# Gathering an expert's tokens straight into the transposed operand, in a hybrid decoder block with a mixture of experts

## The reference

```
h = rms_norm(x, g_ffn)
logits = h @ w_router + b_router             # 32 experts
top 4 of them, weights = softmax over the 4
per expert e, for the tokens that chose it:
    g = min(h @ w_gate[e] + b_gate[e], 7);  u = clip(h @ w_up[e] + b_up[e], -7, 7)
    y += weight * ((g * sigmoid(1.702 g) * (u + 1)) @ w_down[e] + b_down[e])
out = rms_norm(x + y, g_final)
```

## Time and profile before

| | us |
|---|---|
| median of 3 runs | 1185.95 (1185.67 to 1188.35) |
| the profiled execution | 1186.93 |
| its span (first to last record) | 1185.2 |
| TensorE busy | 1120.0 (95%) |
| TensorE weight loads | 539.5 (46%) |
| VectorE, ScalarE, GpSimd busy | 356.0, 227.4, 123.8 |

### The profile page before, as it was taken

The page is one execution under the profiler, slowest core; times in us unless marked ns, Lnnn a source line. Parts: engine busy times, 40 slices in busy tenths (PEclk is TensorE's granted clock), DMA queues, the critical chain, the costliest instruction groups (busy, mean ns, idle before and its releaser), DMA issues.

```text
span 1185.2 us, 14843 instructions
## 1 busy us (share of the span) xinstructions
PE 1120.0 (95%) x5876; PEld 539.5 (46%) x5876; DVE 356.0 (30%) x623; ACT 227.4 (19%) x398; POOL 123.8 (10%) x94
## 2 busy tenths in 40 slices
PE   9899999999999999999999999999999999999896
PEld 7899998983333333333333333333333333333232
DVE  6967786842111111211111111111111111111121
ACT  5456656431001000100100000000000000000001
POOL 4453444420000000000000000000000000000000
PEclk9999999999999999999999998999999999999999
DMA  8454657899999999999999999999999999999994
GB/s 286 143 170 148 222 185 286 290 403 369 431 427 429 426 429 427 428 427 430 426 428 430 426 429 427 429 425 431 425 429 427 427 430 427 431 427 428 429 425 195
DMA packets 71836, 447.63 MB, mean 378 GB/s; under 512 B 5625, under 2 KB 45909, under 8 KB 46709
## 3 DMA queue, kind: packets, MB, share of 16 engines
q1 hardware_dynamic: 71520, 446.94, 91.7%
q10 hardware_dynamic: 277, 0.12, 0.0%
HBM read 445.59 MB, written 1.05 MB: 377 GB/s over the span
## 4 chain that ended last, share of the span: by engine, by line
PE 54%; DMA 34%; DVE 5%; issue 3%; ACT 2%; POOL 0%; SPq 0%; DVEq 0%; ACTq 0%; POOLq 0%
PE psum L746 33%; DMA ring<-in_w_up 29%; DMA ring<-in_w_down 4%; PE psum L759 4%; PE psum L477 3%; PE psum L491 3%; PE psum L711 2%; PE psum L772 1%; PE psum L481 1%; PE psum L495 1%; PE psum L719 1%; DMA ring<-in_w_out 1%; ACT work L1068 1%; DVE work L1293 1%; DVE work L1296 1%
## 5 line engine op out<-in xcount | busy, mean ns | idle before, releaser
L746 PE MATMUL psum<-ring,work 128*64 128x512 f32 x3072 | 687.5, 597 | 45.6 <-DMA ring<-in_w_gate 19.4
L746 PEld LDWEIGHTS psum<-ring,work 128*64 128x64 f32 x3072 | 215.8, 137 | 473.6 <-issue 380.2
L1377 DVE TENSOR_SCALAR work<-psum 128x512 f32<-128x512 f32 x32 | 22.1, 692 | 416.0 <-PE psum L746 416.0
L1516 POOL TENSOR_TENSOR w<-ring,w 128x1024 fp32r<-128x1024 f32 x38 | 101.2, 2668 | 108.7 <-ACT w L925 107.0
L1543 POOL COPY chosen<-pick 96x64 bf16 (+1 forms) x32 | 7.5, 235 | 872.1 <-PE psum L772 872.1
L1382 DVE TENSOR_SCALAR work<-psum 128x512 f32<-128x512 f32 x32 | 22.1, 692 | 226.0 <-PE psum L746 226.0
L1068 ACT COPY work<-psum 128x512 f32<-128x512 f32 x32 | 18.8, 586 | 332.2 <-PE psum L772 332.2
L1152 DVE TENSOR_TENSOR w<-ring,w 128x1024 fp32r<-128x1024 f32 x38 | 72.8, 1917 | 27.5 <-ACT w L925 27.1
L925 ACT CAST w<-ring 128x1024 fp32r<-128x1024 f32 x74 | 74.2, 1049 | 28.6 <-PE psum L481 15.8
L1077 ACT ACTIVATE work<-work 128x512 f32<-128x512 f32 x32 | 20.1, 630 | 256.7 <-DVE work L1377 256.7
L477 PE MATMUL psum<-hh,w 128*128 128x256 f32 x512 | 68.7, 288 | 0.0
(11 more groups left out here) (196 smaller groups left out, 804.4 us busy)
## 6 DMA issues: line engine op xcount, KB each, us to landing
ring<-in_w_up SPq DMA_DIRECT2D x64, 2048.0 KB, 40.8
ring<-in_w_gate SPq DMA_DIRECT2D x63, 2048.0 KB, 43.1
ring<-in_w_down SPq DMA_DIRECT2D x61, 2048.0 KB, 43.1
ring<-in_w_in SPq DMA_DIRECT2D x26, 1024.0 KB, 5.0
ring<-in_w_down SPq DMA_DIRECT2D x6, 1024.0 KB, 40.1
ring<-in_w_conv_o SPq DMA_DIRECT2D x4, 1024.0 KB, 5.1
ring<-in_w_attn_o SPq DMA_DIRECT2D x4, 1024.0 KB, 5.4
ring<-in_w_out SPq DMA_DIRECT2D x4, 1024.0 KB, 7.5
```

What stands on the lines that cost most here:

```text
L746: mm = pe.matmul(psum[64 * h:64 * h + 64, b, :], src[:, k, :], w[:, k2, h * 512:(h + 1) * 512], start=(bias_of is None and k == 0), stop=( ...
L1377: v.tensor_scalar(gm, psum[:, 4, :], LIMIT, None, ALU.min).then_inc(gmin_ready, 1)
L1516: g.tensor_tensor(wL[:, par, 0, :, :], slot(s).rearrange("p (k n) -> p k n", k=KB)[:, :, 0:P], wH[:, par, 0, :, :].bitcast(F32), ALU.subtr ...
```

## The change

1. **Gather.** x is now the stationary operand (128 tokens x 128 columns with a step of 8 elements) and `Gr` the moving one (64 columns), once for each k and each 128 tokens. The result is already transposed, so `rows`, ScalarE's copy (`take_rows`) and `turn_xe` are gone, and VectorE multiplies by the gain straight from the gather's bank. In an expert's turn the first half (k 0 to 3) stands behind `turn_weights`, the second half between the two slots of the down product. In expert 0 the first half stands ahead of `turn_act`. In the last pair the whole gather stands behind the up product. The first gather of all has its halves in banks 6 and 5, each with its own semaphore.
2. **First one-hot.** It is built from the rank sums in PSUM and `Mr0`, the mask times rstd, ahead of `pos`. The subtraction for the exponentials goes behind the mask.
3. **Order at the start.** `turn_wgt` goes between the gate and the up product of expert 0, and two of the residual products between those of expert 1.
4. **Halves.** HALVED gets slots 11, 188 and 190; the refill of slot 11 is issued by halves as slot 10's.
5. **Last pair.** `turn_weights` of the last expert goes with `turn_act`, between the two down slots of the expert before; VectorE's copy of it waits for the scatter.
6. **The end.** Four stores of 256 KB; ScalarE scales three of the quarters, VectorE makes gain and scale of the fourth in one operation from PSUM.

```diff
-HALVED = (EP, RING, NE * EP - 3, NE * EP - 1)
+HALVED = (EP, RING, RING + 1, NE * EP - 4, NE * EP - 3, NE * EP - 2, NE * EP - 1)
...
-                        if first and p == RING and s == 0:
-                            sp.wait_ge(half_used, 1)
+                        if first and p in (RING, RING + 1) and s == 0:
+                            sp.wait_ge(half_used, p + 1 - RING)
                             return True
...
             for t in range(TT):
-                sp.wait_ge(out_ready[t], 1)
-                sp.dma_start(out[0, t * P:(t + 1) * P, :], normed[:, t, :]).then_inc(out_done, 16)
+                for h in range(2):
+                    sp.wait_ge(out_ready[t][h], 1)
+                    sp.dma_start(out[0, t * P:(t + 1) * P, h * 512:(h + 1) * 512],
+                                 normed[:, t, h * 512:(h + 1) * 512]).then_inc(out_done, 16)
...
-            residual(0, 1)
-
-            def gather(nth):
+
+            def gather(nth, halves=range(RUNS), banks=(6, 6)):
 
                 pe.wait_ge(Gr_ready, nth + 1)
-                for t in range(TT):
-                    x_runs = xres[:, t, :].rearrange("p (i h r) -> p i h r", h=RUNS, r=RUN)
-                    for h in range(RUNS):
-                        mm = pe.matmul(psum[64 * h:64 * h + 64, 6, :].rearrange("p (i r) -> p i r", r=RUN), Gr[:, t, :],
-                                       x_runs[:, :, h, :], start=(t == 0), stop=(t == TT - 1), tile_position=(0, 64 * h))
-                mm.then_inc(gathered, 1)
+                for h in halves:
+                    for k in range(RUN * h, RUN * h + RUN):
+                        for t in range(TT):
+                            mm = pe.matmul(bank(banks[h], k * CW, CW), xres[:, t, :].rearrange("p (i k) -> p i k", k=KB)[:, :, k],
+                                           Gr[:, t, :], start=(t == 0), stop=(t == TT - 1))
+                    if banks[0] != banks[1] and h == 0:
+                        mm.then_inc(half_gathered, 1)
+                if RUNS - 1 in halves:
+                    mm.then_inc(gathered, 1)
...
                 wide(4, xe, c * EP, uses, 0, base)
-                gather(j + 1)
+                if at(j, 0):
+                    turn_wgt()
+                if at(j, 1):
+                    residual(0, 1)
+                    residual(1, 1)
+                wide(5, xe, c * EP + RUNS, uses, 1, base)
                 if at(j, 0):
                     pe.wait_ge(wT_ready, 1)
-                wide(5, xe, c * EP + RUNS, uses, 1, base)
-                turn_xe(j + 1)
-                if not at(j, 0):
+                    gather(j + 1, range(1))
+                else:
                     scatter(j, j)
...
                 turn_act(j)
                 turn_weights(j)
+                if not at(j, 0):
+                    gather(j + 1, range(1))
                 pe.wait_ge(aT_ready, j + 1)
                 if not at(j, 0):
                     pe.wait_ge(ysb_ready, j)
-                wide(7, aT, c * EP + 2 * RUNS, uses, None, base)
-
-            gather(0)
-            residual(1, 1)
-            turn_xe(0)
-            turn_wgt()
+                wide(7, aT, c * EP + 2 * RUNS, uses, None, base, lambda: gather(j + 1, range(1, RUNS)))
+
+            gather(0, banks=(6, 5))
...
                 wide(4, xe, 0, uses, 0, base)
+                wide(5, xe, RUNS, uses, 1, base)
                 gather(b)
-                wide(5, xe, RUNS, uses, 1, base)
-                turn_xe(b)
                 scatter(a, a)
...
-                wide(7, aT, 4 * RUNS, uses, None, base, lambda: turn_act(b))
+
+                def turn_last():
+                    turn_act(b)
+                    turn_weights(b)
+
+                wide(7, aT, 4 * RUNS, uses, None, base, turn_last)
                 scatter(b, b)
-                turn_weights(b)
...
+            steps.link(v.tensor_tensor(Mr0, Mb[:, :, 0:1].rearrange("p t e -> p (t e)"), small[:, 10:12], ALU.mult))
             dve.wait_ge(ranks_ready, 1)
+            for t in range(TT):
+                ins = v.tensor_scalar(Gr[:, t, :], count_up, psum[:, 7, 64 + t * NE:65 + t * NE], Mr0[:, t:t + 1], ALU.is_equal,
+                                      ALU.mult)
+            ins.then_inc(Gr_ready, 1)
...
             def take_xe(nth):
 
-                dve.wait_ge(xe_turned, nth + 1)
-                for h in range(RUNS):
-                    to, turned, gain = gained(h)
-                    ins = v.tensor_tensor(to, turned, gain.unsqueeze(2).broadcast_to([P, RUN, CW]), ALU.mult)
-                ins.then_inc(xe_ready, 1)
...
+                dve.wait_ge(gathered, nth + 1)
+                v.tensor_tensor(xe, psum[:, 6, :].rearrange("p (k c) -> p k c", k=KB), g2k[:, :].unsqueeze(2).broadcast_to([P, KB, CW]),
+                                ALU.mult).then_inc(xe_ready, 1)
...
+                if j == NE - 1:
+                    dve.wait_ge(scattered, 4 * NE)
                 take_weights(j)
...
             times_gain(0)
             mean_square(0)
             times_gain(1)
+            mean_square(1)
             times_gain(2)
-            mean_square(1)
-            times_gain(3)
             dve.wait_ge(rstd_ready, RSTD0 + 2)
-            dve.wait_ge(x2g_ready, 4)
-            v.tensor_scalar(normed[:, 1, :], normed[:, 1, :], small[:, 53:54], None, ALU.mult).then_inc(out_ready[1], 1)
+            v.scalar_tensor_tensor(normed[:, 1, 512:D], psum[:, 3, :], small[:, 53:54], gbc[:, 512:D], ALU.mult,
+                                   ALU.mult).then_inc(out_ready[1][1], 1)
```

More of the change, by code:

```diff
@@ L211, in hybrid_block @@
         aT_last = work[:, 4096:4608].rearrange("p (k c) -> p k c", k=KB)
-        rows = work[:, 4096:4608]
         bdn = cst[0:NE, C_SPENT:C_SPENT + D]
@@ L228, in hybrid_block @@
         Gr = work[:, 4712:4840].rearrange("p (t c) -> p t c", t=TT)
+        Mr0 = work[:, 4994:4996]
         posT = work[0:NE, 4096:4096 + T]
@@ L286, in hybrid_block @@
         gfin_in, x2g_ready, out_done = sem("gfin_in"), sem("x2g_ready"), sem("out_done")
-        out_ready = [sem(f"out_ready{t}") for t in range(TT)]
+        out_ready = [[sem(f"out_ready{t}{h}") for h in range(2)] for t in range(TT)]
         def pieces(w):
@@ L748, in wide @@
                                            tile_position=(0, 64 * h))
-                        if base == 0 and p == 0 and k2 == RUN // 2 - 1:
+                        if base == 0 and p in (0, 1) and k2 == RUN // 2 - 1:
                             mm.then_inc(half_used, 1)
@@ L779, in turn_wgt @@
                 for t in range(TT):
-                    tr = pe.transpose(bank(5, t * P, P)[0:NE], wgt[:, t, 0:NE], ident)
+                    tr = pe.transpose(bank(6, t * P, P)[0:NE], wgt[:, t, 0:NE], ident)
                 tr.then_inc(wT_turned, 1)
@@ L1031, in _ @@
             sum_high(NKV - 1)
-            def take_rows(nth):
-                act_e.wait_ge(gathered, nth + 1)
-                nc.scalar.copy(rows, psum[:, 6, :]).then_inc(rows_ready, 1)
             def split_piece(n):
@@ L1077, in squash @@
                 nc.scalar.activation(sg, gm, ACT.Sigmoid, scale=ALPHA).then_inc(sig_ready, 1)
-            take_rows(0)
             act_e.wait_ge(wT_turned, 1)
-            nc.scalar.copy(wT[:, :], psum[0:NE, 5, 0:256]).then_inc(wT_ready, 1)
+            nc.scalar.copy(wT[:, :], psum[0:NE, 6, 0:256]).then_inc(wT_ready, 1)
             for j in range(UNROLL):
                 squash(j)
-                take_rows(j + 1)
                 take_act(j)
@@ L1114, in _ @@
                                      accum_out=small[:, 44 + b:45 + b]).then_inc(ssq_ready, 1)
-            act_e.wait_ge(rstd_ready, RSTD0 + 1)
-            act_e.wait_ge(x2g_ready, 2)
-            nc.scalar.activation(normed[:, 0, :], normed[:, 0, :], ACT.Copy, scale=small[:, 52:53]).then_inc(out_ready[0], 1)
+            for t, h in ((0, 0), (0, 1), (1, 0)):
+                act_e.wait_ge(rstd_ready, RSTD0 + t + 1)
+                act_e.wait_ge(x2g_ready, 2 * t + h + 1)
+                done = normed[:, t, h * 512:(h + 1) * 512]
+                nc.scalar.activation(done, done, ACT.Copy, scale=small[:, 52 + t:53 + t]).then_inc(out_ready[t][h], 1)
         @block.vector
@@ L1340, in _ @@
             steps.link(ins)
-            v.tensor_tensor(below, lg, top8[:, :, 0:1].broadcast_to([P, TT, NE]), ALU.subtract).then_inc(shifted_ready, 1)
             steps.link(v.memset(top8[:, :, TOPK:8], MASKED))
@@ L1346, in _ @@
             v.tensor_tensor(Mb[:, :, :], less4[:, :, TOPK:TOPK + NE], lg, ALU.not_equal).then_inc(M_ready, 1)
+            v.tensor_tensor(below, lg, top8[:, :, 0:1].broadcast_to([P, TT, NE]), ALU.subtract).then_inc(shifted_ready, 1)
             dve.wait_ge(M_ready, 1)
+            steps.link(v.tensor_tensor(Mr0, Mb[:, :, 0:1].rearrange("p t e -> p (t e)"), small[:, 10:12], ALU.mult))
             dve.wait_ge(ranks_ready, 1)
+            for t in range(TT):
```

(27 more changed lines are left out.)

13 lines of the change are left out of this document (2 added, 11 removed).

## The result

The changed kernel takes 1343.26 us (median of 4 runs, 1342.62 to 1344.93) against 1185.98 before: a ratio of 1.132, 95% interval 1.130 to 1.134. The prediction was 1185.7 with a range to 1197. It is wrong by 158 us, and in the direction of its first rival.

What follows compares the result with a forecast made beforehand. The prediction took the DMA stream of expert weights to set the end, with TensorE nearly as long. Its terms, -0.5 (stream) + 0.7 (last pair) - 0.5 (end) = -0.3 us, gave 1185.7 us, range 1182 to 1197.

Steps and rivals of the forecast that it cites:

- rival 1: Expert stage: strided x loads take over 0.125 us, TensorE never catches up and becomes the bound; 1200 to 1268; chance 0.28.
- 32 x 0.12 = 3.84 us: New gather, per expert: 32 weight loads of strided x at 0.12 us each, priced near the 16-byte transposes.
- The upper end: Gather loads: 0.213 us each, if a 32-byte step makes a load take two turns; chance 0.08 for loads near it.
- the forecast's own period: TensorE's time for one expert without DMA waits: 26.93 before, 28.1 us forecast with the new gather.
- Whether TensorE catches up: Expert stage: TensorE's lag of 32.5 us at expert 1 shrinks 1.27 an expert, caught up after 25.6 experts.
- The edge: Expert stage: the longest period at which TensorE still catches up, 28.25 us, or a load of 0.125 us.
- the prediction's rule of 9.3 us per 0.01: Expert stage, past the edge: each 0.01 us more a load costs 29 x 0.32 = 9.3 us.
- First product at 267.2: Start: expert 0's first product begins at 267.2 us instead of 267.65, 0.45 sooner.
- The stream's start (-0.5): Start of the weight stream: sooner refills of the slots gain 0.5 us, bounds -2.9 to +0.8.
- Rival 2: Stream's start: halved refills and sooner ups close the whole gap; about -3.9 us in all, 1182; chance 0.21.
- The last pair (+0.7): Experts 30 and 31: TensorE's work behind expert 30's second up slot (1131.8) ends at 1175.0 instead of 1174.3.
- The end (-0.5, bounds +0.4 to -0.9): Final scales and stores: four stores leave 256 KB behind the last issue instead of 512, gaining 0.5 us.

Runs made afterwards that it cites:

- experiment 4: A kernel of its own, fp32 matmul groups with stationary operands at different steps between bf16 matmuls: 0.118 us a load at step 1, 0.241 at 8; transposes 0.12 at 8.
- experiment 2: The changed kernel with gate and up weights reordered so the gather's stationary operand steps 16 bytes instead of 32: 1332.3 us, ratio 1.124.
- experiment 1: The changed kernel with the gather's stationary operand taking 128 columns of x side by side (other columns than the weights belong to): 1187.22 us, ratio 1.0005.
- experiment 8: The contiguous variant of experiment 1 with k-blocks 0 and 1 of each expert's gather done twice, 8 more loads: 1206.38 us, ratio 1.0155.
- 5: The changed kernel with one-hot columns repeated up to four times (up to 256 moving columns) in the expert loop's gather: 1310.53 us, ratio 1.104.
- 6: The changed kernel with gate and up weights laid out for a step of 8 bytes in x, DMA rows 8 KB instead of 16: 1195.97 us, ratio 1.0070.
- experiment 3: The kernel before plus the change without its gather, only one residual product moved and `turn_wgt` in its old place: 1185.38 us against 1186.36, ratio 0.9993.

## Why the prediction was wrong

**The step that failed** is the term "32 x 0.12 = 3.84 us". It measured 0.24 a load, 7.8 us an expert. Its mistake was in the choice of the nearest row. Transposes at a 16-byte step were taken to speak for the same step in a matmul; experiment 4 shows both operations at one step, 0.12 against 0.24. The upper end, twice the contiguous load (0.213), had nearly the right size, though it was put on a step of 32 bytes alone and experiment 2 shows it at 16 as well; it got a chance of 0.08. The Trainium skill (SBUF — State Buffer, Specifications (TRN2)) asks for two hits in each 16-byte line. The prediction read the transposes as evidence against it, and for fp32 matmuls the runs agree with it: a step of 2 (two elements to a line) is nearly free (0.123 against 0.118), 3 costs half more, 4 and up about double. The same page's section "Door 1: The DMA port swizzle" lets four fp32 be stepped for free; at that step the load took 0.236 us, so here the measurement decides.

**The rest of that step was nearly right.** With 0.24 put in, the forecast's own period is 28.1 + 3.84 = 31.9; measured 31.87. Contiguous it was 27.82, not 28.1: less the loads, 24.06 is left in both kernels (31.87 - 7.81 and 27.82 - 3.76, start to start) where the forecast had 24.3, so its other terms were 0.2 too high together.

**Whether TensorE catches up** was the right question. At 0.12 it does: the chain goes over to the weights 24 experts after expert 1, where 25.6 were forecast. The edge was put at 28.25 and is at 28.08; period and edge were both forecast a little high, and by luck the two cancelled.

**What rival 1 left out** is the clock, and what the step costs outside the 28 experts. Against experiment 1, the same kernel without the step, the span is 156.0 us longer. In the 28 experts 28 x (31.87 - 27.82) = 113.4 are the loads; 7.2 of it only fill the waits for weights that experiment 1 still had, and 106.2 remain, where the prediction's rule of 9.3 us per 0.01 gives 29 x (31.94 - 28.25) = 107. The slots at the low clock are 18 x 1.69 = 30.4, and the period with the bias spread takes 0.2 off. Ahead of scatter 0 it is 9.5 more (322.90 against 313.36), behind scatter 28 10.0 more (88.4 against 78.4); there loads and clock are not told apart. So with 0.24 for a load rival 1's rule comes to 1185.7 + 107 = 1293, and the other 50 us are the clock and the two ends.

**First product at 267.2:** it came at 271.96, and at 268.62 even in experiment 1. There the 32 loads took 5.06 us with a granted clock of 0.77 in these 10 us, and the product behind them 8.72 instead of 6.87. Experiment 8 has the same first gather and a clock of 1.00 over it: 3.71 us, and the first product stands at 267.17, where it was forecast. First experiment 1, then experiment 8:

```profile
260.00:270.00 10.00, 9.24 (x50) 6.61 (x51) 5.27 (x29) 0.74 (x2) 0.63 (x2) 0.77 0.96 402
...
263.13 5.13 PE L712 MATMUL psum<-work,xres 128*128 128x64 f32 x32 [0.72 <-DVE work L1345]
268.62 8.78 PE L743 MATMUL psum<-ring,work 128*64 128x512 f32 x32
```

```profile
260.00:270.00 10.00, 9.25 (x61) 5.86 (x62) 6.08 (x32) 0.84 (x2) 0.72 (x2) 1.00 0.99 406
...
263.22 3.79 PE L713 MATMUL psum<-work,xres 128*128 128x64 f32 x32 [0.72 <-DVE work L1346]
267.17 7.04 PE L744 MATMUL psum<-ring,work 128*64 128x512 f32 x32
```

What makes the clock fall there in one and not in the other is open. It is no accident of one run: from 265 to 270 us the granted clock is 0.50 to 0.65 in the changed kernel and in experiments 1, 2, 5 and 6, and 1.00 in experiment 8 and in both kernels with the old gather.

**The stream's start (-0.5)** is best judged in experiment 8, whose first product stands at the forecast time (its first gather half in expert 0 has the 0.9 us of added loads). From 270 to 300 us it moves 370, 439 and 395 GB/s against 334, 406 and 390 before: 0.74 MB more, 1.7 us gained. But behind that it gives the same back. First experiment 8, then the kernel before:

```profile
310.00:330.00 20.00, 20.00 (x114) 9.96 (x112) 3.45 (x8) 1.17 (x2) 0.23 (x1) 1.00 0.97 392
...
310.00:330.00 20.00, 19.54 (x95) 7.16 (x96) 4.28 (x11) 2.39 (x4) 0.23 (x1) 1.00 1.01 428
```

From 270 to 330 us together it is even. The reason given in the prediction, that the gap is open again in expert 1, fits; the 0.5 did not come. Over the same 60 us experiment 1, whose first product runs at the low clock, moves 0.6 MB less than the kernel before (1.4 us lost), experiment 3 with the old gather 0.3 MB more (0.7 us gained). Rival 2 was wrong: the gap moved, and did not close.

**The last pair (+0.7)** came as it was worked out. In experiment 1 the second up slot of expert 30 begins at 1132.18 (forecast 1131.8), no product behind it waits for weights, and the last down product ends 43.3 us later (forecast 43.2). That is 1.2 us later than before, of which 0.4 is the slot's own lateness:

```profile
1168.36 7.09 PE L743 MATMUL psum<-ring,work 128*64 128x512 f32 x32
```

**The end (-0.5, bounds +0.4 to -0.9)** gained more. From the last scatter to the end of the span it is 10.2 us before, 8.7 in the changed kernel and in experiments 1, 2, 5 and 6, 9.8 in experiment 8 and 10.2 in experiment 3, each with the same four stores: 1.5 us gained in five profiles of seven. The term that was too small is the store's size: one of 256 KB lands 2.2 us after its issue in experiment 1, one of 512 KB before took 4.0, and 0.65 had been put for it. In the other two the stores begin as soon (4.2 us behind the last scatter), but issuing the four takes 2.64 and 2.98 us instead of 2.05, and they land after 3.0 and 3.2; why is not settled.

## What to carry to other kernels

Price an operand by its own operation and its own step: a strided row of a transpose says nothing of a strided fp32 matmul operand. Where a price has two ends a factor of two apart and the margin lies just above the lower one, the chance of the upper end is what the forecast hangs on, and a rule that names a mechanism weighs more than a row of another operation. When TensorE waits for its loads, look at the product behind it too, since it may run at the lower clock.

## What the runs showed that was not expected

- The price of a step fits how many elements share 16 bytes: 0.118, 0.123, 0.185, 0.236 and 0.241 us a load at steps of 1, 2, 3, 4 and 8 fp32. Moving operands behave in the same way (3.62, 3.79, 5.60 and 7.38 us for 16 records at 1 to 4), runs of four are free, and transposes pay next to nothing (1.88, 2.12 and 1.96 us for 16 loads at 1, 4 and 8).
- The slow loads with 64 moving columns were followed by products at the low clock in two of three experts; with up to 256 columns beside the same loads in none, and the kernel was 33 us faster for the added work. What else brings the clock down, as at the first gather of most runs, is open.
- One in 28 periods is longer in every kernel, the one with the down bias (6.9 us in experiment 1, 6.6 in the changed kernel). Its own product takes 3.6 us of that, and the windows behind it show a granted clock of 0.64 and 0.68 (735 to 745 us in experiment 1). The kernel before has it too (0.71 and 0.61 at 725 to 735 us), mostly hidden there by the stream.
- Gate and up weights loaded in rows of 8 KB instead of 16, and in another order, came with 1% less of the stream's rate (424 against 428 GB/s).
